# A down projection as seven block products of sums in place of eight plain ones, on one core of Trainium2

## What is computed

```python
def conv_ffn(h, w_up, conv_w, conv_b, w_down):
    T = h.shape[1]
    u = h @ w_up
    up = jnp.pad(u, ((0, 0), (CONV_WIDTH - 1, 0), (0, 0)))
    c = conv_b + sum(conv_w[i] * up[:, i:i + T] for i in range(CONV_WIDTH))
    gate, val = jnp.split(c, 2, axis=-1)
    return (jax.nn.silu(gate) * val) @ w_down
...
        x = x + conv_ffn(rmsnorm(x, norm2_g[l]), w_up[l], conv_w[l], conv_b[l], w_down[l])
    return rmsnorm(x, normf_g)
```

## Time and profile before

| | us |
|---|---|
| runs: median (lowest to highest, 3 runs) | 1065.77 (1065.23 to 1066.2) |
| profiled execution, its own time | 1065.23 |
| its span, first to last instruction | 1063.6 |
| TensorE busy | 1047.7 (99%) |
| DVE, ScalarE, GpSimd busy | 674.3, 499.4, 130.2 |
| granted TensorE clock, mean | 0.999 |

### The profile page before, as it was taken

How to read it: one execution, slowest core, us unless ns; L and a number is a source line. 1 busy time by engine, 2 the same in 40 slices (tenths; PEclk the granted TensorE clock), 3 DMA queues, 4 the chain that set the end, 5 groups by cost and what they waited for, 6 DMA issues and landing times.

```text
span 1063.6 us, 17993 instructions
## 1 busy us (share of the span) xinstructions
PE 1047.7 (99%) x6746; PEld 840.0 (79%) x6746; DVE 674.3 (63%) x1158; ACT 499.4 (47%) x859; POOL 130.2 (12%) x195
## 2 busy tenths in 40 slices
PE   8999999999999999999999999999999999999997
PEld 7887888777777777777777888888888888888886
DVE  5224655587988878878776445557777777752234
ACT  6426675633534445335444333565565556531122
POOL 8100000220220321313210110100000000000000
PEclk9999999999999999999999999999999999999999
DMA  7632322321211313314242553423333333323321
GB/s 205 157 95 84 95 85 83 97 62 41 63 35 59 95 49 83 81 50 117 74 145 88 150 158 118 139 81 99 99 93 103 88 99 90 99 99 99 99 80 79
DMA packets 156087, 101.48 MB, mean 95 GB/s; under 512 B 31369, under 2 KB 144311, under 8 KB 156023
## 3 DMA queue, kind: packets, MB, share of 16 engines
q1 hardware_dynamic: 148800, 79.72, 25.5%
q0 software_dynamic: 7072, 20.83, 7.3%
q10 hardware_dynamic: 151, 0.04, 0.0%
HBM read 91.65 MB, written 8.91 MB: 95 GB/s over the span
## 4 chain that ended last, share of the span: by engine, by line
PE 93%; DVE 3%; ACT 2%; issue 1%; DMA 1%; ACTq 0%; POOL 0%; DVEq 0%
PE ps L1749 16%; PE ps L1751 15%; PE ps L1752 15%; PE ps L1705 5%; PE ps L1707 4%; PE ps L1706 4%; PE ps L2253 4%; PE ps L2252 4%; PE ps L2254 4%; PE ps L1887 3%; PE ps L2014 2%; PE ps L2035 2%; PE ps L1831 1%; PE ps L1967 1%; PE ps L1944 1%; PE ps L1924 1%
## 5 line engine op out<-in xcount | busy, mean ns | idle before, releaser
L1165 DVE TENSOR_TENSOR wlo<-raw,whi 128x1024 fp32r<-128x1024 f32 x128 | 156.7, 1224 | 206.7 <-ACT whi L764 137.0
L764 ACT ACTIVATE whi<-raw 128x1024 fp32r<-128x1024 f32 x124 | 131.1, 1057 | 111.3 <-PE ps L1752 108.5
L1749 PE MATMUL ps<-xnh,whi 128*128 128x512 f32 x344 | 133.9, 389 | 0.0
L1752 PE MATMUL ps<-xnh,wlo 128*128 128x512 f32 x344 | 133.8, 389 | 0.0
L1751 PE MATMUL ps<-xnl,whi 128*128 128x512 f32 x344 | 133.8, 389 | 0.0
L1749 PE MATMUL ps<-xh,whi 128*128 128x512 f32 x248 | 98.7, 398 | 1.0 <-DVE xl L1183 1.0
L1751 PE MATMUL ps<-xl,whi 128*128 128x512 f32 x248 | 96.8, 390 | 0.0
L1752 PE MATMUL ps<-xh,wlo 128*128 128x512 f32 x248 | 96.5, 389 | 0.0
L1705 PE MATMUL ps<-xh,whi 128*128 128x512 f32 x184 | 85.2, 463 | 0.4 <-DVE wlo L1165 0.4
L1751 PEld LDWEIGHTS ps<-xnl,whi 128*128 128x128 f32 x344 | 64.6, 188 | 13.5
L1749 PEld LDWEIGHTS ps<-xnh,whi 128*128 128x128 f32 x344 | 64.6, 188 | 13.4
(11 more groups left out here) (358 smaller groups left out, 2203.3 us busy)
## 6 DMA issues: line engine op xcount, KB each, us to landing
raw<-in_w_in SPq DMA_DIRECT2D x108, 256.0 KB, 3.1
raw<-in_w_up SPq DMA_DIRECT2D x88, 256.0 KB, 3.0
raw<-in_w_down SPq DMA_DIRECT2D x44, 256.0 KB, 2.8
gates_scratch<-gst POOLq DMA_DIRECT2D x16, 256.0 KB, 3.2
raw<-in_w_proj_b SPq DMA_DIRECT2D x16, 256.0 KB, 3.8
raw<-in_w_proj_a SPq DMA_DIRECT2D x16, 256.0 KB, 3.0
gl<-gates_scratch POOLq DMA_DIRECT2D x16, 256.0 KB, 3.1
raw<-in_w_out SPq DMA_DIRECT2D x16, 256.0 KB, 2.9
```

Source lines behind the costliest of these rows:

```text
L764: act.activation(flat(whi[:, hb]), flat(raw[:, b]), ACT.Copy).then_inc(w_hi, 1)
L1165: dve.tensor_tensor(flat(lo[:, hb]), flat(raw[:, b]), flat(hi[:, hb]).bitcast(F32), ALU.subtract).then_inc(w_lo, 1)
L1749: pe.matmul(ps[bank][:, :], whi[:, hb, k, :], hi(k), start=first and k == 0, stop=False)
L1752: ins = pe.matmul(ps[bank][:, :], wlo[:, hb, k, :], hi(k), start=False, stop=last and k == kn - 1)
```

## The change

The result is seen as 2 x 2 blocks (tokens 0 to 255 and 256 to 511; columns 0 to 511 and 512 to 1023), and the 2816 rows as two halves of 11 slices. In place of eight block products, each of 11 slices x 2 token blocks x 3 terms, seven are made, of sums and differences of blocks.

- *Weights.* In UP, GpSimd loads two slices of `w_down` (k and 11 + k) per turn, makes four sums of 512 columns (L810 to L818) and stores them in `weight_scratch` in HBM, from where SP loads them in DOWN as any other weight (`load_down`). Slice 0's sums are made at the start of UP.
- *Hidden.* UP's tiles come in another order, so that a turn gives slices i and 11 + i. DVE writes the product of gate and value straight into `ha` and `hb`; the copy into `hh` and the subtraction into `hl` are gone from UP. GpSimd makes four sums of 256 tokens per turn (`hidden_sums`, L826 to L831).
- *DOWN.* The high and low parts of the hidden sums are made slice by slice in DOWN, in two buffers each (`split_hidden`, ScalarE L898, DVE L1765). TensorE runs a first part of 11 stages with four products (two weight tiles, 24 matmuls a stage), a second of 11 stages with two products (12 matmuls each) and a third with the last product, 11 slices in 6 weight tiles. All tiles use `whi` and `whx` in turn, four buffers.
- *Putting together.* ScalarE copies four banks out of PSUM after the first part, DVE adds two banks to two of these and two more to the sums; GpSimd adds the shared parts and the residual to what each block still needs (12 sums of 512), DVE adds banks to that at the end of the second and third part. Blocks 2 and 3 are done after the second part, 0 and 1 after the third.

```diff
+            def weight_sums(k):
+                if k:
+                    pool.wait_ge(wsum_stored, 48 * k)
+                for i in range(2):
+                    pool.dma_start(wrow[:, i], w_down_v[i * FH + k]).then_inc(wrow_in, 16)
+                pool.wait_ge(wrow_in, 32 * (k + 1))
+                chain(pool.tensor_tensor(wdiff[:, :], wrow[:, 0, 1, :], wrow[:, 0, 0, :],
+                                         ALU.subtract))
+                pool.dma_start(wsum[k][:, 0], wdiff[:, :]).then_inc(wsum_stored, 16)
...
+            pool.wait_ge(slot_done, N_UP)
+            weight_sums(0)
+            for i in range(FH):
+                if i < FH - 1:
+                    weight_sums(i + 1)
+                hidden_sums(i)
...
+            def split_hidden(i):
+                if i < FH:
+                    act.wait_ge(hsum_ready, i + 1)
+                if i == 0:
+                    act.wait_ge(wsum_stored, 48 * FH)
+                elif i == 1:
+                    act.wait_ge(h_ready, FT)
+                else:
+                    act.wait_ge(slot_done, N_DOWN + (2 * i - 2 if i - 2 < FH else i + 10))
+                act.activation(hidden(hsh[i % 2], i), hidden_source(i), ACT.Copy).then_inc(hs_hi, 1)
...
             table(ACT.Sqrt)
-            for u in range(2, FT):
-                split_down(u)
+            for k in range(FH):
+                split_down(2 * k + 2)
+                split_hidden(k + 1)
+                split_down(2 * k + 3)
...
                     if u % 2:
                         dve.wait_ge(conv_done, i * 4 + u + 1)
-                        dve.wait_ge(silu_ready, j + 1)
-                        dve.tensor_tensor(cv[:, :], cv[:, :], cg[:, :], ALU.mult)\
-                            .then_inc(h_ready, 1)
-                        dve.wait_ge(hh_ready, j + 1)
-                        dve.tensor_tensor(hl[:, bass.ds(j, 1), :], cv[:, :],
-                                          hh[:, bass.ds(j, 1), :].bitcast(F32),
-                                          ALU.subtract).then_inc(hl_ready, 1)
+                        dve.wait_ge(silu_ready, i * 2 + u // 2 + 1)
...
+            for k in range(FH):
+                for side in range(2):
+                    t = 2 * k + side
+                    pe.wait_ge(w_lo, N_DOWN + t + 1)
+                    pe.wait_ge(hs_lo, k + 1)
+                    for wcol, hcol, bank in (((0, 0, FIRST), (1, 3, SECOND)),
+                                             ((0, 1, THIRD), (1, 2, PAIRED)))[side]:
+                        if k == 0 and bank == PAIRED:
+                            pe.wait_ge(ps_free, N_DOWN)
+                        for half in range(2):
+                            ins = down(t, wcol, k, hcol, bank, half, start=k == 0,
+                                       stop=k == FH - 1)
```

More of the change, by code:

```diff
@@ L755, in _ @@
+            for i in range(2):
+                pool.tensor_tensor(blocks(yt[:, i, T:D]), blocks(yt[:, i, T:D]),
+                                   residual(i, 1), ALU.add).then_inc(rest_ready, 1)
         @block.scalar
@@ L1111, in _, with up_tiles @@
                 x1_turned(m)
[L1113 removed]
+            def up_tiles(i, last=False):
                 for u in range(4):
[L1115 removed]
+                    n, j = i * 4 + N_UP + u, i + u // 2 * FH
                     split(n + 2, u % RAW, u % 2)
@@ L1137, in rms, with squares @@
                                bias=eps_col[:, 0:1]).then_inc(y_rms, 1)
[L1139 to L1147, removed]
+            def squares(j, part, cols):
+                act.activation(junk3[:, j, cols], yt[:, j, cols], ACT.Square, scale=D ** -0.5,
+                               accum_out=parts[:, 4 * j + part:4 * j + part + 1])\
+                    .then_inc(y_sq, 1)
@@ new lines, in _ @@
+            for k in range(16):
+                if k < 15:
+                    split_down(2 * FH + 2 + k)
+                split_hidden(FH + 1 + k)
+                if k in (12, 13):
+                    j = k - 10
+                    act.wait_ge(y_sum, j + 1)
+                    act.wait_ge(rest_ready, j + 3)
+                    chain(act.activation(junk2[:, :], yt[:, j, :], ACT.Square,
+                                         accum_out=stat[:, j:j + 1]))
+                    rms(j)
+                if k == 14:
+                    for j in range(2):
+                        squares(j, 0, slice(0, T))
@@ new lines, in up_tiles @@
+                        dve.tensor_tensor(dst.rearrange("p o a b -> p (o a) b"),
+                                          cv[:, :].rearrange("p (a b) -> p a b", a=2),
+                                          cg[:, :].rearrange("p (a b) -> p a b", a=2),
+                                          ALU.mult).then_inc(h_ready, 1)
+                    if last and u == 1:
+                        split_hidden(0)
+            with chain.loop(FH - 1, 4) as i:
+                up_tiles(i)
+            up_tiles(FH - 1, last=True)
@@ new lines, in _ @@
+            for j in range(2):
+                gained(j, slice(0, T))
+            dve.wait_ge(y_sq, 2)
+            dve.tensor_scalar(parts[:, 2:3], parts[:, 0:1], 1e-6, None, ALU.add)\
+                .then_inc(y_total, 1)
+            dve.wait_ge(y_done, 4)
+            dve.wait_ge(rest_ready, 8)
+            dve.tensor_tensor(yt[:, 0, T:D], ps[THIRD][:, :], yt[:, 0, T:D], ALU.add)\
+                .then_inc(y_sum, 1)
+            dve.wait_ge(y_sum, 5)
+            gained(0, slice(T, D))
@@ new lines, in _ @@
+            pe.wait_ge(rs_ready, 1)
+            pe.wait_ge(x1t_ready, KT)
+            for k in range(FH):
+                for side in range(2):
[9 more added lines that the diff above has]
+                                       stop=k == FH - 1)
+                            if k == FH - 1 and (half == 0 or bank in (FIRST, THIRD)):
+                                ins.then_inc(first_done, 1)
+                    ins.then_inc(slot_done, 1)
@@ new lines, in _ @@
+            for k in range(FH):
+                t, i = 2 * FH + k, FH + k
+                pe.wait_ge(w_lo, N_DOWN + t + 1)
+                pe.wait_ge(hs_lo, i + 1)
+                for side, bank in enumerate((FIRST, SECOND)):
+                    for half in range(2):
+                        if k == 0:
+                            pe.wait_ge(copied, 2 * side + half + 1)
+                        ins = down(t, side, i, side, bank, half, start=k == 0,
+                                   stop=k == FH - 1)
+                        if k == FH - 1 and (bank, half) != (SECOND, 1):
+                            ins.then_inc(y_done, 1)
+                ins.then_inc(slot_done, 1)
```

335 lines of the change are left out of this document (232 added, 103 removed).

## The result

The changed kernel takes **1093.0 us** (median of 4 runs, 1092.6 to 1093.5) against 1065.5 for the kernel before on the same chip: ratio 1.026, 95% interval 1.024 to 1.0275. It is slower, as forecast, but by 27.5 us where 10 were forecast, and outside the range (1057 to 1086).

The account below looks back on a forecast made before the run. TensorE's matmul count was taken to bound the kernel, plus waits the change creates and the tail: 1065.2 - 15.0 + 7.8 + 0.6 + 12 + 5 = 1075.6, forecast 1076 us; range 1057 to 1086 (forecast's own cases 1068 to 1090).

Parts of the forecast that it names:

- Removed, -15.0: DOWN: 462 matmuls in place of 528, 66 fewer at 0.2267 us, all on the critical path, -15.0 us.
- The engines exclude each other both ways: GpSimd and DVE operations reading SBUF, two operands on DVE: each can make the other wait; basis of the +12 and +5.
- the first rival: DVE is never held, GpSimd only waits for it; 1059 us (1056 to 1062), faster than before; chance 0.30.
- whoever starts first holds the other: SBUF port shared by DVE and GpSimd: the operation that starts first holds it for the whole instruction.
- GpSimd in UP, +12 (5 to 22): UP: GpSimd's sums hold DVE's two-operand operations and make TensorE wait, +12 us (5 to 22).
- its upper end: UP: a pair of tiles takes 11.9 us against 10.88, 1.0 too long, 22 us in 22 pairs.
- gets in only where DVE has a gap: UP: GpSimd not between two DVE operations in a row, half the hold; pair 10.6 us, only crowded tiles stall, some 5 us.
- Seams of DOWN, +7.8: UP to DOWN and between DOWN's parts: queue order makes ScalarE and DVE late for TensorE, +7.8 us (6 to 10).
- the hold there, +5: Seams and DOWN's second part: GpSimd's sums delay tile 1 and DVE's low halves, +5 us (4 to 10).
- Second to third part: DOWN: four more sums stand behind hidden split 23 with stages of only 2.72 us; +0.3, +1.4, +0.6.
- Tail, +0.6: After the last matmul: ScalarE's scaling of 1024 for block 0 stands before the last squares, +0.6 us (0 to 1.2).
- Transfers at nothing: DOWN: loads at 193 GB/s fit the buffers' 10.9 us round, cost 0; rival of late transfers +5 us, chance 0.03.

Follow-up runs that it names:

- the run without them: Changed kernel with weight sums and sums of UP's outputs left out and DOWN's twelve output sums replaced by fills; 1060.1 us (0.9949 of before).
- the table: One turn each of four kernels: changed (1093.0 us), without sums of UP's outputs (1085.8), weight sums without their traffic (1082.5), weight sums waiting for TensorE's tiles (1091.4).
- moving one such wait: Changed kernel with ScalarE in UP waiting for DVE's odd-tile product only before writing the buffer it reads, not before splitting the next weights; 1063.7 us (0.9987 of before).
- the kernel with the tied sums: Changed kernel with GpSimd's four weight sums per turn waiting for TensorE's second, third, third and fourth tiles; 1091.4 us (1.0244 of before).

## Why the prediction was right and wrong

- **Removed, -15.0:** right; 66 matmuls fewer at 0.2267 us.
- **The engines exclude each other both ways:** right. The row that the first rival named as deciding is there in every turn: DVE's low-half subtraction begun inside a GpSimd sum (853.72, sum to 854.18) takes 1.54 for 1.23. That whoever starts first holds the other, as the prediction has it, these rows don't bear out: two of the three large holds fall on operations that start before the sum.
- **GpSimd in UP, +12 (5 to 22): this step failed.** It is +25.1. The working behind its upper end was 2 x 9.3 us of chain and 5.2 us of hold in a turn, 22 us in all. The hold was over-estimated (3.9), but the chain was 20.3 and not 18.6: I read it from a pair of tiles without the table load, though every turn has one in front of its first pair's copy, in the kernel before too:

```profile
878.45 1.28 ACT L764 ACT_TABLE_LOAD   x1
```

  Then I took a value near half of the upper end, for the case that GpSimd "gets in only where DVE has a gap". It doesn't stop there: three operations in a row are held, since GpSimd has its next sum ready while DVE's current operation runs. With 20.3 + 3.9 - 21.76 = 2.46 us per turn, ten turns give 24.6 of the 25.1.
- **Seams of DOWN, +7.8, and the hold there, +5:** 17.0 in place of 12.8. The largest was sized exactly: 4.7 before DOWN's second stage, measured 4.67; with the 0.58 at tile 1 5.25 against 5.0. Second to third part 0.18 + 1.14 + 0.18 = 1.5 against 2.3. Between the first part and there 2.28 + 0.50 + 0.95 + 0.92, = 4.65, mostly the hold by the sums of outputs: 7.3 us by the run without them against the 5, the half clock behind the first included. These nine waits are 11.4 us. Not foreseen at all were two stretches at half clock, about 3 us together (the second behind the 2.28), and some 0.2 to 0.3 us around each wait: at the first of them the matmuls start 0.97 us apart, with 0.58 in the bracket.
- **Tail, +0.6:** +0.3 measured.
- **Transfers at nothing:** right, though the blocks of 256 KB take 3.4 us to land in place of 2.8.

Not tried: the weight sums on DVE, and GpSimd sums placed by a wait on DVE's own progress. Open: which engine goes first, and what makes the clock fall.

## What to carry to other kernels

Before work is put on an idle GpSimd, count which operations of VectorE read two SBUF operands, and expect each GpSimd sum that meets one to hold it for up to the sum's whole length, also several in a row: here GpSimd's sums held VectorE for 2.9 to 4.7 us in the turns of the table, depending on what they met. Then compare the whole loop's chain through the helping engines, table loads and waits included, with TensorE's time per turn; a page with TensorE at 99% says nothing about how thin that cover is (1.4 us of 21.8). Where it is too thin, look for a wait that stands earlier than the buffer it protects: moving one such wait won 29 us, where the one other placement of the sums on GpSimd that was tried won 1.6.

## What the hardware showed beyond the forecast

- **Half clock behind a wait of a few us.** The kernel before holds its clock at 1.00 through UP and DOWN. In the changed one it falls to 0.50 (1.2 GHz) after some waits of TensorE. Windows just behind the change of stages (PEclk is the third number from the end):

```profile
974.00:976.00 2.00, 1.73 (x4) 1.47 (x5) 2.00 (x3) 1.93 (x3) 0.00 (x0) 0.50 0.72 253
976.00:978.00 2.00, 2.00 (x7) 1.55 (x7) 2.00 (x3) 0.00 (x0) 0.00 (x0) 0.67 0.73 192
```

  Behind the 4.67 us wait eight matmuls take 3.33 us from start to start in place of 1.81 (974.27 to 977.60): 1.5 us more. It also fell after waits of 2.72, 2.28, 1.85 and 1.82 us, but not after others of 1.82 to 2.04, and none of 1.14 us or less was followed by it. The length of the wait alone doesn't tell: in the kernel with the tied sums, three waits of 2.63 us were followed by it (those before 820.75, 868.82 and 916.90) and one was not (before 795.75). In UP it cost nothing: turns with and without such a stretch last the same 24.2 us, because TensorE wasn't what bound them; the next wait is shorter instead (0.52 in place of 1.8 us).
- **Perfect alternation.** In the rows of DOWN above, where both engines have the next operation ready, they take strict turns, and each row lasts its own time and its wait for the other: 1.78 and 2.31 us on DVE for 0.69 and 1.23, 1.1 more each; on GpSimd 1.62 and 2.28 for 1.3, so 0.3 and 1.0 more. GpSimd's fill of 1450 elements (1.3 us), which reads nothing, is not part of this.
